# Sums of squares of q and k as two fp32r products of a rounded high part and a low part, issued after the sixth of eight product steps

## What is computed

```
h = rmsnorm(x);  proj = h @ w_in           # aq, ak, av, xq among its columns
q = rmsnorm(aq per head of 64, q_norm_g);  k = rmsnorm(ak per head of 64, k_norm_g)
xq = rmsnorm(xq per head of 128);          k_mem = rmsnorm((rmsnorm(mem) @ w_mem_kv)[k] per head of 128)
rmsnorm(t, g) = t * rsqrt(mean(t*t) + eps) * g
```

## Time and profile before

| | us |
|---|---|
| median of three runs | 2518.88 |
| lowest and highest | 2518.37, 2520.21 |
| the profiled execution, its own time | 2520.59 |
| its span, first to last instruction | 2518.9 |
| TensorE busy in the span | 2347.6 (93%) |
| VectorE, ScalarE, GpSimd busy | 1210.1, 914.3, 476.5 |
| mean granted TensorE clock | 0.961 of full speed |

### The profile page before, as it was taken

How to read it: one execution, slowest core, us unless ns; L and a number is a source line. 1 busy time by engine, 2 the same in 40 slices (tenths; PEclk the granted TensorE clock), 3 DMA queues, 4 the chain that set the end, 5 groups by cost and what they waited for, 6 DMA issues and landing times. The chain is left out here.

```text
span 2518.9 us, 36506 instructions
## 1 busy us (share of the span) xinstructions
PE 2347.6 (93%) x14401; PEld 2059.0 (82%) x14401; DVE 1210.1 (48%) x1742; ACT 914.3 (36%) x1456; POOL 476.5 (19%) x297
## 2 busy tenths in 40 slices
PE   5999998999799999999989979749999999999997
PEld 4877775666688888888868858649999999999997
DVE  6334446445433231000144443567767766676673
ACT  6334344444500002211120032245555555555552
POOL 0001111110300000000000000043444443444443
PEclk6999998998999999999989989869999999999998
DMA  5310000001011102232245454278888887888882
GB/s 176 100 34 18 26 26 17 18 26 42 1 43 42 39 27 84 76 94 75 77 144 163 138 191 147 96 256 270 256 282 269 276 268 242 273 273 282 262 273 54
DMA packets 328100, 343.47 MB, mean 136 GB/s; under 512 B 11664, under 2 KB 308624, under 8 KB 327440
## 3 DMA queue, kind: packets, MB, share of 16 engines
q1 hardware_dynamic: 315280, 309.96, 38.9%
q0 software_dynamic: 12672, 31.46, 4.7%
HBM read 297.35 MB, written 44.04 MB: 136 GB/s over the span
## 5 line engine op out<-in xcount | busy, mean ns | idle before, releaser
L2104 PE MATMUL bank_pair<-tokens_hi_lo,ehi 128*128 128x320 f32 x2048 | 536.4, 348 | 6.0 <-DVE tokens_hi_lo L1941 3.3
L2105 PE MATMUL bank_pair<-tokens_hi_lo,elo 128*128 128x160 f32 x2048 | 484.8, 237 | 0.0
L1860 ACT ACTIVATE ehi<-eraw 128x2048 fp32r<-128x2048 f32 x192 | 364.6, 1907 | 85.0 <-PE bank_pair L2105 66.5
L2105 PEld LDWEIGHTS bank_pair<-tokens_hi_lo,elo 128*128 128x128 f32 x2048 | 394.0, 192 | 0.0
L2104 PEld LDWEIGHTS bank_pair<-tokens_hi_lo,ehi 128*128 128x128 f32 x2048 | 387.1, 189 | 6.6 <-issue 6.6
L1930 DVE TENSOR_TENSOR elo<-eraw,ehi 128x2048 fp32r<-128x2048 f32 x141 | 331.7, 2352 | 25.2 <-ACT ehi L1860 20.8
L1834 POOL TENSOR_TENSOR elo<-eraw,ehi 128x2048 fp32r<-128x2048 f32 x47 | 235.6, 5012 | 380.7 <-ACT ehi L1860 380.7
L2104 PE MATMUL bank_pair<-hidden_hi_lo,ehi 128*128 128x320 f32 x1024 | 265.3, 346 | 0.0
L2105 PE MATMUL bank_pair<-hidden_hi_lo,elo 128*128 128x160 f32 x1024 | 241.3, 236 | 0.0
L1242 PE MATMUL bank_pair<-hT_hi,whi 128*128 128x512 f32 (+1 forms) x576 | 204.0, 354 | 1.2 <-PEq L1072 1.2
L1243 PE MATMUL bank_pair<-hT_lo,whi 128*128 128x512 f32 (+1 forms) x576 | 204.0, 354 | 0.0
(11 more groups left out here) (265 smaller groups left out, 4088.9 us busy)
## 6 DMA issues: line engine op xcount, KB each, us to landing
eraw<-in_w_eg SPq DMA_DIRECT2D x64, 1024.0 KB, 6.9
eraw<-in_w_eu SPq DMA_DIRECT2D x64, 1024.0 KB, 6.4
eraw<-in_w_ed SPq DMA_DIRECT2D x64, 1024.0 KB, 5.9
raw<-in_w_in SPq DMA_DIRECT2D x64, 512.0 KB, 4.1
scratch_g<-sig SPq DMA_DIRECT2D x24, 640.0 KB, 3.4
sig<-scratch_g SPq DMA_DIRECT2D x24, 640.0 KB, 3.9
xt<-in_x SPq DMA_DIRECT2D x10, 512.0 KB, 4.5
scratch_m<-acc SPq DMA_DIRECT2D x8, 640.0 KB, 4.8
```

The lines of the kernel that those rows point to most:

```text
L1860: nc.scalar.activation(ehi[j % NES][:], eraw[j % NER][:], ACT.Copy).then_inc(e_hi, 1)
L2104: nc.tensor.matmul(out, wh, moving[:, k, :], start=(k == 0), stop=False)
L2105: ins = nc.tensor.matmul(out[:, HI], wl, moving[:, k, HI], start=False, stop=(k == KD - 1))
```

## The change

The square is written twice by ScalarE: unrounded into `sq`, and rounded to fp32r into one tile `sq_hi`. GpSimd subtracts one from the other and puts the low part, as fp32r, in the place of `sq`. TensorE sums by two fp32r products that accumulate, ones by high and ones by low. The sums are issued after the sixth product step, behind `amid`, where before they were issued after the second, ahead of `amid`. ScalarE takes `amid` and `split_hi` ahead of the logarithm and exponential; VectorE takes `split_lo` ahead of `finish`; GpSimd takes its unit steps tick by tick with the subtraction between those of `amid` and of `after`. Tiles move 1664 bytes down to make room for `sq_hi`. No DMA is added or moved.

```diff
-    HT = 6400
+    HT = 4736
+    sq_lo = [at(f"sq_lo{i}", [P, 512], F32R, W + 70656 + 2048 * i) for i in range(2)]
+    sq_hi = at("sq_hi", [P, 512], F32R, W + 84992)
...
             for t, tk in enumerate(ticks):
                 s = tk["seg"]
+                for what, v in tk["amid"]:
+                    if what == "scores":
+                        exps(v)
+                    elif what == "values":
+                        o_copy(v)
+                if s is not None and segs[s]["first"]:
+                    split_hi(segs[s]["chunk"] + 1)
                 if t >= 1 and t - 1 < NSEG and t - 1 in norm_no:
...
-                for what, v in tk["amid"]:
-                    if what == "scores":
-                        exps(v)
-                    elif what == "values":
-                        o_copy(v)
-                if s is not None and segs[s]["first"]:
-                    split_hi(segs[s]["chunk"] + 1)
...
                                          ACT.Square).then_inc(sq_ready, 1)
+                    if norm_no[s] >= 1:
+                        act.wait_ge(ss_done, norm_no[s])
+                    nc.scalar.activation(sq_hi[:, 0:sg["nt"]], bank[s % 3][:, 0:sg["nt"]],
+                                         ACT.Square).then_inc(sq_hi_ready, 1)
...
+            def square_lo(m):
+                nt = segs[norm_segs[m]]["nt"]
+                pool.wait_ge(sq_ready, m + 1)
+                pool.wait_ge(sq_hi_ready, m + 1)
+                nc.gpsimd.tensor_tensor(sq_lo[m % 2][:, 0:nt], sq[m % 2][:, 0:nt], sq_hi[:, 0:nt].bitcast(F32),
+                                        ALU.subtract).then_inc(sq_lo_ready, 1)
+            for tk in ticks:
+                for what, v in tk["amid"]:
+                    if what == "scores":
+                        probabilities(v)
+                if tk["seg"] in norm_no:
+                    square_lo(norm_no[tk["seg"]])
+                for what, v in tk["after"]:
+                    if what == "scores":
+                        probabilities(v)
...
                 units_steps(tk["amid"])
+                if s is not None and segs[s]["first"]:
+                    split_lo(segs[s]["chunk"] + 1)
                 if t >= 1 and t - 1 < NSEG:
                     finish(t - 1)
-                if s is not None and segs[s]["first"]:
-                    split_lo(segs[s]["chunk"] + 1)
...
-                pe.wait_ge(sq_ready, m + 1)
+                pe.wait_ge(sq_lo_ready, m + 1)
...
-                nc.tensor.matmul(misc[:, 0:sg["nt"]], w[:], sq[m % 2][:, 0:sg["nt"]], start=True,
+                w = w[:].bitcast(F32R)
+                nc.tensor.matmul(misc[:, 0:sg["nt"]], w, sq_hi[:, 0:sg["nt"]], start=True, stop=False)
+                nc.tensor.matmul(misc[:, 0:sg["nt"]], w, sq_lo[m % 2][:, 0:sg["nt"]], start=False,
                                  stop=True).then_inc(ss_done, 1)
...
                     product(tk["seg"], range(MID))
-                if t >= 1 and t - 1 in norm_no:
-                    square_sums(t - 1)
                 units_steps(tk["amid"])
                 two = len(tk["rounds"]) > 1 and tk["seg"] is not None
+                sums = t >= 1 and t - 1 in norm_no
+                if tk["seg"] is not None and (two or sums):
+                    product(tk["seg"], range(MID, LATE))
+                if sums:
+                    square_sums(t - 1)
                 if two:
-                    product(tk["seg"], range(MID, LATE))
                     v_round(rounds_done[0])
                     rounds_done[0] += 1
                 if tk["seg"] is not None:
-                    product(tk["seg"], range(LATE if two else MID, KD))
+                    product(tk["seg"], range(LATE if two or sums else MID, KD))
```

More of the change, by code:

```diff
@@ L180, in kernel_body @@
     lse = small("lse", 6)
-    assert o <= 6400, o
-    HT = 6400
+    HT = 4736
+    assert o <= HT, o
     hT_hi = at("hT_hi", [P, KD, NT], F32R, HT)
@@ L428, in kernel_body @@
     sq_ready = sem("sq_ready")
+    sq_hi_ready = sem("sq_hi_ready")
+    sq_lo_ready = sem("sq_lo_ready")
     ss_done = sem("ss_done")
@@ L677, in _, with probabilities @@
         def _(pool):
-            for v in range(n_units):
+            def probabilities(v):
                 un = unit(v)
```

## The result

The changed kernel took 2556.05 us, median of four runs (2553.08 to 2561.05), against 2518.62 for before beside it: a ratio of 1.0151 [1.0132, 1.0170], 37.4 us slower. The forecast was 9.1 us slower, range 2514 to 2541: the sign was right, the size four times too small, and the range missed. The profiled execution took 2554.22, with a span of 2552.4 against 2518.9.

A forecast was written before the change was run, and what follows sets the result against it. TensorE was taken to bound the straight stage nearly everywhere, with little to spare. The terms +3.0 - 6.7 - 2.7 - 3.2 + 0.5 made it 9.1 us slower: 2518.9 + 9.1 = 2528.0 us, range 2514 to 2541.

The forecast's parts named there:

- The sums on TensorE: Two fp32r products cost 0.46 us (0.24 for 256 tokens) instead of 0.86 (0.43); at most 17.4 us saved.
- Added work: ScalarE's second square 0.60 and 0.36 us, GpSimd's subtraction 1.04 and 0.61; 0.4 waited in ticks 11 and 14.
- Ticks without units: Ticks 1 to 4, 9 to 14 except 12's size, and 18: cheaper sums gain 3.0 us in all.
- `finish` becomes late: Ticks 17 and 19 to 68 outside the first combining: VectorE's work queues behind a late `finish`; together 6.7 us lost.
- The two combinings: Chains of VectorE and ScalarE, where a delay counts in full: 2.7 us lost in the first, 3.2 in the second.
- The lock: GpSimd's subtraction and VectorE's `split_lo` exclude each other; not expected to meet; as rival up to 18.7 us more, 2544, chance 0.03.
- The clock: Rival: added waits in two-round ticks and combinings bring one or two more stretches below full clock; 2540 us, chance 0.07.
- five rivals: Whole saving 2502 (0.15), unit waits cancel 2521 (0.20), clock 2540 (0.07), lock 2544 (0.03), products at float32 price 2583 (0.02).

The follow-up runs named there:

- combining step first: Changed kernel with VectorE's combining step ahead of `finish` in ticks 45 to 47 and 69 to 71; 2540.72 us, ratio 1.0095.
- fillers: Changed kernel with unused product instructions added on TensorE ahead of the sums of ticks 47 and 71 and the broadcasts of tick 48; 2553.79 us.
- high part twice: Changed kernel without GpSimd's subtraction, the second product of each sum taking the rounded high part again; 2544.79 us, ratio 1.0100.
- copy of v first: Changed kernel with VectorE's copy of v ahead of `split_lo`, `finish` staying behind it; 2542.94 us, ratio 1.0090.
- `finish` last: Changed kernel with copies of v ahead of `split_lo` and `finish` at its tick's end, except ahead of the last combining step in ticks 48 and 72; 2514.72 us.
- routing's wait: `finish` last version with GpSimd's four subtractions of the first expert's weights waiting until VectorE has packed the prompt's lists; 2507.37 us, ratio 0.9954.

## Why the prediction was right in sign and wrong in size

- **The sums on TensorE:** right, 0.46 to 0.48 and 0.24 us a pair. That the 17.4 us would mostly not reach the end was right too; 2.6 did by the profiles, and none by the total times.
- **Added work:** the squares as forecast; the subtraction 0.23 longer than I took and outside my bounds. It cost 0.5 in ticks 11 and 14, where 0.4 stood.
- **Ticks without units:** -2.6 against -3.0.
- **`finish` becomes late:** the mechanism and its places are those forecast (vT, `lse_copy`, the maxima), and the two-round ticks lose 1.4 to 1.7 each where 1.15 stood. The other ticks were summed too kindly: ticks 30 and 31 lose 1.1 us where I had 0.1, because `pv` waits 1.20 for `lse_copy` there too. From 19 to 68, the first combining left out, the table has 18.6 us against 6.0 forecast; 3.5 of that lie in tick 50, in the wake of the combining, and 2.4 are half clock in ticks 33 and 36 of that one execution.
- **The two combinings:** this is the step that failed most. In the first I priced the wait ahead of its broadcasts in tick 48 and 0.7 us for the longer chain, -2.7, in the second the delay of its first step, -3.2, and took the steps between as unchanged. Ticks 46 to 48 and 69 to 72 lose 14 us where 5.9 stood, and 17.4 with tick 50. The first broadcasts came 4.2 us later, counted as forecast, where I had named 2.7, the second 5.2 where I had 3.2. In the run with the combining step first, 46 to 50 and 69 to 72 together come out 14.3 us better: each maximum, sum and weight of VectorE stood behind its own late `finish`, and the squares of the next segment behind ScalarE's exponentials of the combining, so that the sums of ticks 47 and 71 waited 6.7 and 5.7 us.
- **The lock:** I looked for it at `split_lo`, where it cost 0.3 us in six ticks without units, and counted nothing for VectorE's own steps of the combinings. There the subtractions met a maximum or sum four times, about 1 us each; without the subtraction the two combinings lose 3.9 us less.
- **The clock:** held at 0.07 as a rival. It came beside the forecast's losses, not in place of them; the first combining's share is some 3 us by the one profile with fillers. None of the five rivals gives 2556 either.
- **Not in the working:** the routing, 6.2 us. "Nothing outside the straight stage is edited" was true, and yet time was lost there, because a meeting of two engines depends on when they arrive. With that meeting excluded in both kernels the loss is 2548.26 - 2519.38 = 28.9 us, which is the straight stage's 29.7 within the scatter.

What is still open is how much of the unit ticks' loss is clock in an average execution: the records of two executions of the same instructions differ by 2.4 us there.

## What to carry to other kernels

When a result is issued later, list what stands behind its consumer on each in-order engine, and move the consumer behind the work that needs nothing of it: the same change lost 29.7 us of the straight stage with `finish` in its old turn and won 12.5 (9.5 in a second profile) with it at the end of the tick and the copies of v ahead of `split_lo`. A chain of dependent steps on one engine pays for a late instruction at every step that is queued behind one, so price each step and not the first. A saving on the engine that looks busiest is worth what the next wait lets through, here next to nothing of 17.4 us in one order and 8 to 11 in the other.

## What the runs showed of the hardware that was not expected

VectorE's 16x32 copies and scalar operations, 0.16 us alone, took 4.5 us when they began under a GpSimd subtraction, one whole subtraction each, while the maxima and searches of the same lists ran on beside it unhindered. From none to three such hits were seen in one execution (none in before, three with the high part twice and with the copy of v first), and that stage took from 64.0 to 75.5 us. The Trainium skill, "SBUF — State Buffer", section "Who interferes with whom", says that copies and scalar operations in their two-port modes take the shared ports for the whole instruction as well as two-input ones do; the trace agrees, at 4.49 to 4.56 us a hit, though it does not show the mode that these instructions ran in, and I had used the half of that rule on two inputs alone.

TensorE's clock was granted in full in one execution and partly at half in another over the same instructions with the same waits ahead (ticks 33 and 36: a grant of 0.82 and 0.83 against 1.00). With `finish` last tick 50 differs in the same way: 9.67 us at a grant of 1.00, and 12.10 at 0.72 in the version with the routing's wait. So a half-clock stretch in one profile is not yet a cost of the change.
